# Turning the attention weights of heads 0 to 5 on DVE and through DRAM, and summing squares on ACT, in a two-layer attention and recurrence kernel

## The reference

```python
q, k, v, gate = jnp.split(rms_norm(h) @ w_in, 4, axis=-1)
q, k = rms_norm(q per head), rms_norm(k per head)
z = q @ k.T * scale                      # 128 queries x up to 1024 keys
log_beta = log_sigmoid(z)
log_skip_j = where(causal, log_sigmoid(-z), 0.0)
log_skip = cumsum(log_skip_j, reverse=True) - log_skip_j
weights = where(causal, exp(log_beta + log_skip), 0.0)
o = weights @ v
h = h + (o * silu(gate)) @ w_out
```

## Time and profile before

| | |
|---|---|
| Median of 3 runs | 1175.18 us (1175.09 to 1175.25) |
| Span of the profiled execution | 1173.5 us |
| PE busy | 1163.8 us, 99% of the span |
| DVE busy | 796.7 us, 68% |
| ACT busy | 419.7 us, 36% |
| POOL busy | 149.8 us, 13% |
| DMA traffic | 113.51 MB |

### The profile page before, as it was taken

The page is one execution under the profiler, slowest core; times in us unless marked ns, Lnnn a source line. Parts: engine busy times, 40 slices in busy tenths (PEclk is TensorE's granted clock), DMA queues, the critical chain, the costliest instruction groups (busy, mean ns, idle before and its releaser), DMA issues. The chain is left out here.

```text
span 1173.5 us, 20148 instructions
## 1 busy us (share of the span) xinstructions
PE 1163.8 (99%) x7228; PEld 1071.4 (91%) x7228; DVE 796.7 (68%) x1612; ACT 419.7 (36%) x911; POOL 149.8 (13%) x344
## 2 busy tenths in 40 slices
PE   8999999999999999999999999999999999999998
PEld 8999999999999999888888989898999999999787
DVE  5757485766767675774444778788888888788421
ACT  5535353545445454452222222323232322222200
POOL 2422121203031211110003100000000000000000
PEclk9999999999999999999999999999999999999999
DMA  8210223223142301066632110314142421117441
GB/s 251 57 53 19 73 82 112 68 83 103 67 119 73 109 1 46 1 228 218 209 108 73 55 36 20 115 66 137 70 145 72 133 86 45 45 37 296 148 139 72
DMA packets 110659, 113.51 MB, mean 97 GB/s; under 512 B 6880, under 2 KB 86752, under 8 KB 110560
## 3 DMA queue, kind: packets, MB, share of 16 engines
q1 hardware_dynamic: 110560, 112.23, 30.1%
HBM read 79.70 MB, written 32.51 MB: 96 GB/s over the span
## 5 line engine op out<-in xcount | busy, mean ns | idle before, releaser
L28 PE MATMUL p_proj<-w_qkv_hi,ut_hi 128*128 128x384 f32 x504 | 172.0, 341 | 0.2 <-DVE ut_lo L796 0.2
L30 PE MATMUL p_proj<-w_qkv_hi,ut_lo 128*128 128x384 f32 x504 | 169.1, 336 | 0.0
L29 PE MATMUL p_proj<-w_qkv_lo,ut_hi 128*128 128x384 f32 x504 | 168.7, 335 | 0.0
L28 PE MATMUL p_proj<-w_ig_hi,next_hi 128*128 128x256 f32 x512 | 145.5, 284 | 0.0
L29 PE MATMUL p_proj<-w_ig_lo,next_hi 128*128 128x256 f32 x512 | 143.1, 279 | 0.0
L30 PE MATMUL p_proj<-w_ig_hi,next_lo 128*128 128x256 f32 x512 | 143.0, 279 | 0.0
L28 PE MATMUL p_proj<-next_hi,w_qf_hi 128*128 128x512 f32 x282 | 113.2, 402 | 0.0
L30 PE MATMUL p_proj<-next_hi,w_qf_lo 128*128 128x512 f32 x282 | 110.1, 390 | 0.0
L29 PE MATMUL p_proj<-next_lo,w_qf_hi 128*128 128x512 f32 x282 | 109.8, 390 | 0.0
L808 DVE TENSOR_TENSOR_SCAN a_skip<-a_skip,a_diagonal 128x129 f32<-128x129 f32 (+3 forms) x64 | 86.9, 1358 | 30.2 <-ACT a_beta L648 28.4
L28 PEld LDWEIGHTS p_proj<-w_ig_hi,next_hi 128*128 128x128 f32 x512 | 96.2, 188 | 0.0
(11 more groups left out here) (255 smaller groups left out, 2732.3 us busy)
## 6 DMA issues: line engine op xcount, KB each, us to landing
stage<-in_hg_w_in_dram SPq DMA_DIRECT2D x32, 512.0 KB, 4.3
stage<-in_sb_w_in_dram SPq DMA_DIRECT2D x29, 512.0 KB, 5.9
w_out_hi_scratch<-m_in SPq DMA_DIRECT2D x32, 256.0 KB, 2.1
w_out_lo_scratch<-m_in SPq DMA_DIRECT2D x32, 256.0 KB, 2.3
m_in<-mixed_scratch SPq DMA_DIRECT2D x12, 448.0 KB, 6.1
a_beta<-in_x_dram SPq DMA_DIRECT2D x8, 512.0 KB, 4.3
m_in<-in_sb_w_out_dram SPq DMA_DIRECT2D x16, 256.0 KB, 3.6
ut_hi<-w_out_hi_scratch SPq DMA_DIRECT2D x8, 512.0 KB, 8.7
```

Of the source, the lines that this page charges most:

```text
L28: pe.matmul(out, w_hi, m_hi, start=start, stop=False, skip_group_check=True)
L29: pe.matmul(out, w_hi, m_lo, start=False, stop=False, skip_group_check=True)
L30: return pe.matmul(out, w_lo, m_hi, start=False, stop=stop, skip_group_check=True)
```

## The change

In heads 0 to 5 PE no longer transposes the weights. After `weigh`, DVE transposes each 32 by 32 square in place within its partitions (`flip`, a STREAM_TRANSPOSE of (i+1)*128 columns into `skip[i % 2]`). SP (`carry`) stores that in DRAM, waits until it has landed, and loads it back in four transfers, one for each group of 32 partitions, in an order that finishes the transposition, over the buffer that `beta` was in. Two steps later ACT copies the high part (`settle_weights`) and DVE makes the low part (`refine_weights`), both from SBUF. There are three `beta` buffers in place of two, and the sigmoids of tile i wait for the low part of tile i-3. `wt_hi` and `wt_lo` have another layout: a block of 128 query columns is now read as four runs of 32. Outputs move by a step or more, to the middle of the projections of steps 4, 6, 8 and of step 0 of the next head (`mid`). Heads 6 and 7 still turn their weights on PE, in the new layout.

The sums of squares move, for all heads, from DVE to ACT (`square_raw`: two Square activations of 128 columns, each of which waits for the one before), and k is scaled in place. The loads of the weight columns from head 2 on move from SP's queue to ACT's. The halves of the output weights are split at steps 1, 2, 4, 5 in place of 5, 6, 7, 9.

```diff
     PLAIN = {"before": {i: [("scores", 0, i)] for i in range(TILES)},
-             "after": {i: ([("outputs", 0, (i - 3) // 2)] if i >= 3 and i % 2 == 1 else []) +
-                       ([("turn", 0, i - 1)] if 1 <= i <= TILES else []) for i in range(USES)}}
+             "mid": {i: ([("outputs", 0, i // 2 - 2)] if i >= 4 and i % 2 == 0 else []) +
+                        ([("settle", 0, i - 2)] if i >= 2 else [("outputs", -1, PAIRS - 1)] if i == 0 else [])
+                     for i in range(USES)},
+             "after": {}}
...
-    SPLIT_AT = [5, 6, 7, 9]
+    SPLIT_AT = [1, 2, 4, 5]
+    OUTPUTS_AT = KT // 2
...
+            def carry(h, j, group):
+
+                sp.wait_ge(flipped, TILES * h + j + 1)
+                run = (j + 1) * QUARTER
+                sp.dma_start(flips[j, :, 0:4 * run], skip[j % 2][:, 0:4 * run]).then_inc(flip_stored[j % 2], 16)
+                sp.wait_ge(flip_stored[j % 2], 16 * (PAIRS * h + j // 2 + 1))
+                for c in range(4):
...
+                    sp.dma_start(flipped_blocks(h, j)[c * QUARTER:(c + 1) * QUARTER, :, :],
+                                 flips[j, :, c * run:(c + 1) * run].rearrange("(g p) r -> p g r", g=4)
+                                 ).then_inc(carried[j % 3], 16)
...
-                        if i >= 2:
-                            act.wait_ge(weights_turned, UNITS * h + ENDS[i - 2])
...
+                            elif i >= 3:
+                                act.wait_ge(wt_ready, UNITS * h + ENDS[i - 3])
...
+            def settle_weights(h, j):
+
+                act.wait_ge(carried[j % 3], 64 * ((3, 3, 2)[j % 3] * h + j // 3 + 1))
+                if j >= 2 or not known_first(h):
+                    act.wait_ge(o_done, PAIRS * h + j // 2)
+                act.activation(slot_of(wt_hi, j), flipped_blocks(h, j), ACT.Copy).then_inc(wt_hi_ready, Z_UNITS[j])
+
+            def square_raw(n, t):
...
+                for part in range(2):
+                    if part == 1 or t >= 1 or not known_first(n):
+                        act.wait_ge(sums_ready, 2 * (NAT * n + t) + part)
+                    act.activation(squares[:, :], raw[t % 4][:, part, :], ACT.Square,
+                                   accum_out=sum_sq[t % 2][:, part:part + 1]).then_inc(sums_ready, 1)
...
+            def flip(h, i):
+
+                width = (i + 1) * P
+                dve.wait_ge(weights_ready, TILES * h + i + 1)
+                dve.transpose(skip[i % 2][:, 0:width].rearrange("p (c s i) -> p s c i", c=4, i=QUARTER),
+                              weights_of(h, i)[:, 0:width].rearrange("p (s c i) -> p s c i", c=4, i=QUARTER)
+                              ).then_inc(flipped, 1)
...
+            def refine_weights(h, j):
+
+                dve.wait_ge(wt_hi_ready, UNITS * h + ENDS[j])
+                dve.tensor_tensor(slot_of(wt_lo, j), flipped_blocks(h, j), slot_of(wt_hi, j).bitcast(F32),
+                                  ALU.subtract).then_inc(wt_ready, Z_UNITS[j])
...
+                            if kt == OUTPUTS_AT:
+                                attend(h, b, plan, "mid", i)
```

More of the change, by code:

```diff
@@ L63, in build_trunk, with link @@
         m_in = [sb(f"m_in{i}", [P, HEADS, P]) for i in range(2)]
-        def link(tag):
+        row_loaded = [ctx.enter_context(nc.semaphore(f"row_loaded{r}")) for r in range(HEADS)]
+        def link(tag, layer):
             def sem(name):
@@ L73, in link @@
                     "rows_free": sem("rows_free"),
-                    "row_loaded": [sem(f"row_loaded{r}") for r in range(HEADS)],
+                    "row_loaded": row_loaded,
+                    "row_landed": 32 * (layer + 1),
                     "stored": sem("mixed_stored"),
@@ L385, in build_attention @@
         raw = [sb(f"raw{i}", [P, 3, P]) for i in range(4)]
-        squares = [sb(f"squares{i}", [P, P]) for i in range(2)]
+        squares = sb("squares", [P, P])
         sum_sq = [sb(f"sum_sq{i}", [P, 2]) for i in range(2)]
@@ L440, in build_attention @@
         weights_ready = sem("weights_ready")
+        flipped = sem("flipped")
+        flip_stored = [sem(f"flip_stored{i}") for i in range(2)]
+        carried = [sem(f"carried{i}") for i in range(3)]
         weights_turned = sem("weights_turned")
@@ L464, in of_head, with of_plan @@
             return (h, b) if d == 0 else (h + d, 1 - b)
+        def of_plan(plan, when, h, i):
+            return [entry for entry in plan[when].get(i, []) if entry[1] >= 0 or not known_first(h)]
         def turn_events(plan, projects, first_head):
@@ L469, in turn_events @@
             for i in range(USES):
-                for when in ("before", "after"):
+                for when in ("before", "mid", "after"):
                     if when == "after" and projects and i >= 3 and i % 2 == 1:
@@ L647, in sigmoids @@
                                    scale=inv_rms[b][i][:, 2:3])
-                    act.activation(beta[i % 2][:, cols], p_z[unit % 3][:, 0:width], ACT.Sigmoid,
+                    act.activation(weights_of(h, i)[:, cols], p_z[unit % 3][:, 0:width], ACT.Sigmoid,
                                    scale=inv_rms[b][i][:, 0:1]).then_inc(sigmoids_ready, 1)
             def attend(h, b, plan, when, i):
-                for what, d, tile in plan[when].get(i, []):
+                for what, d, tile in of_plan(plan, when, h, i):
                     head, half = of_head(h, b, d)
@@ L660, in attend @@
                             copy_weights(head, tile, u, turn_bank(plan, event))
+                    elif what == "settle":
+                        settle_weights(head, tile)
                     elif what == "mixed":
@@ L732, in step @@
                             split_hi(n + 1, p)
+                    if plan is FIRST and i == USES - 1:
+                        for p in range(3):
+                            load(2, p)
                     if plan is SQUEEZED and i == USES - 1:
@@ L743, in step @@
                         gate_sigmoids(n, nb, i, t)
+                    if plan is PLAIN and i == 5:
+                        load(h + 2, 3)
+                    if plan is PLAIN and i == USES - 1 and not (isinstance(h, int) and h == HEADS - 3):
+                        for p in range(3):
+                            load(h + 3, p)
                     if splits_rows(h) and i in SPLIT_AT:
@@ L810, in weigh @@
                 dve.wait_ge(scan_done, TILES * h + i + 1)
[L811 removed]
+                weights = weights_of(h, i)[:, 0:width]
+                dve.tensor_tensor(weights, weights,
                                   skip[i % 2][:, 1:width + 1], ALU.mult).then_inc(weights_ready, 1)
+            def flip(h, i):
[4 more added lines that the diff above has]
+                              ).then_inc(flipped, 1)
             def attend(h, b, plan, when, i):
[L816 removed]
+                order = of_plan(plan, when, h, i)
                 if plan is SQUEEZED and when == "after" and i == USES - 1:
@@ L822, in attend @@
                         weigh(head, tile)
+                        if plan is PLAIN:
+                            flip(head, tile)
+                    elif what == "settle":
+                        refine_weights(head, tile)
                     elif what == "outputs":
```

132 lines of the change are left out of this document (84 added, 48 removed).

## The result

| | before | changed |
|---|---|---|
| Median, same chip | 1175.2 us | 1207.8 us |
| Span of the profiled execution | 1173.5 us | 1206.6 us |
| PE busy | 1163.8 us | 1157.1 us |
| Mean granted clock of PE | 1.00 | 0.983 |

The change makes the kernel slower by a factor of 1.0274 (95% interval 1.026 to 1.0289). The forecast, 1185.7 us with a range from 1160 to 1203, had the direction and missed the size: the added time is 33 us and not 10.5.

A forecast was written before the change was run, and what follows sets the result against it. PE was taken to bound the kernel. 6 x (5.5 waited - 4.0 saved) = +9 us, plus 1.5 for squares: 1173.5 + 10.5 = 1184.0, with the 1.7 around it 1185.7 us; range 1160 to 1203 for 8 in 10.

The forecast's parts named there:

- What PE saves: PE's 36 turns of the weights in a head, 0.11 us each: 4.0 us a head, 23.8 in six heads.
- The chain: Alternating ACT and DVE work, steps 3 to 7: low part of tile 5 at 32.4 us, PE waiting 5.5 a head.
- the forecast's time 0: The end of PE's projection in step 3 of a head, from which the forecast counted its times.
- The rule against it: Low parts on DVE and POOL instructions exclude each other: up to 0.4 us each, 1.6 a head, sum 1195.
- the one on the transfers: Carries through DRAM: tile 4's takes 7 to 8 us where 10.3 are free, so it and SP's wait are hidden.
- The slower PE after each gap: Rival: PE slow behind each gap of 4.5 us, 3 us a head, time 1204; chance 0.07.
- The squares: Squares on ACT in heads -1, 6 and 7, ahead of copies PE needs: 1.5 us, ends 0 and 5.
- The full gain: Rival: flips and squares fit and PE never waits, 1153 us; chance 0.08.
- The signs: If right: PE idle before outputs in steps 6 and 8, ACT waiting before tiles 6 and 7's sigmoids, head of 65 us.
- the signs of an error: If wrong: a head of 59.5 us, ACT's high part waiting on transfers, or granted clock below 1 behind the gaps.

The follow-up runs named there:

- x2_fill: The changed kernel with idle transposes on PE ahead of its wait at outputs 2 of heads 0 to 5: 1193.7 us, ratio 1.016.
- x11: x1_split6 with, on DVE, the low part of tile i-2 made right behind the product of tile i, ahead of the flip: 1156.2 us, ratio 0.9836.
- x12: The kernel before with only the turned weights and the output bank in quarters, outputs reading runs of 32 columns: 1175.9 us, ratio 1.0003.
- x1_split6: The changed kernel with the fourth half of the output weights split at step 6 in place of step 5: 1196.4 us, ratio 1.0178.
- x4: The kernel before with only the sums of squares moved from DVE to ACT, in all heads: 1177.1 us, ratio 1.0016.
- x5: The changed kernel with the sums of squares on DVE again: 1208.6 us, ratio 1.0275.
- x3_out_after: The changed kernel with outputs 1 and 2 at the ends of steps 6 and 8 in place of their middles: 1183.0 us, ratio 1.0058.

## Why the prediction was wrong

Against the head of 60.0 us (56.9 for head 0, which holds no outputs 3), from the windows and the waits of each head:

| head | takes | waits of PE | rest |
|---|---|---|---|
| 0 | 64.88 | 4.7 | 3.3 |
| 1 | 66.50 | 5.0 | 1.5 |
| 2 | 70.30 | 7.6 | 2.7 |
| 3 | 72.24 | 9.8 | 2.4 |
| 4 | 71.16 | 8.2 | 3.0 |
| 5 | 66.22 | 4.7 | 1.5 |
| sum | 411.3 | 40.0 | 14.4 |

Six heads of 63.50 are 381.0 before; without waits and at full clock they would be 356.9, and 3.05 of that difference only moves on, with outputs 3 of head 5, into the next head, which takes 43.09 for 40.04: PE saves 21.0. So -21.0 + 40.0 + 14.4 = 33.4, where the spans differ by 33.1. The rest is half clock: x2_fill keeps the granted clock at 1.00, and about 12.4 us of it go.

The forecast's sum had +10.5. Of the 22.6 us that it missed, 14.4 are PE at half clock, a term that stood in the sum at nothing; 11.6 are longer waits of PE behind a load of output weights, which the sum also had at nothing; and 2.8 are a saving that was counted too high. Against that, the chain's own waits are 4.7 us shorter than forecast, and 1.5 us for the squares does not show.

**What PE saves** was mis-sized: 21.0 us in place of 23.8, 3.5 a head and not 4.0. It was counted from the turns of tiles 6 and 7 alone, and the smaller groups cost less. In the kernel before, in the head from 255.98 us, the turns of tiles 0 to 7 take 0.03, 0.14, 0.27, 0.36, 0.49, 0.57, 0.70 and 0.79 us from the first one's start to the start of the matmul behind them: 3.34 for the 36, 0.093 each and not 0.11. The matmul behind a group is slower as well (0.31 for a gate matmul in place of 0.23), which the forecast's 0.88 for tile 7 includes. Summed from start to start over PE's timeline, a head of x11 spends 0.6 us less on scores than one before, but 0.2 more on outputs and 0.3 more on projections. The layout is at most a small part (x12).

**The chain** held to 0.3 us. In head 5, which has no output weights to split, the matmul behind the projection of step 3 starts at 432.08, which is the forecast's time 0; DVE's timeline gives the low parts of tiles 2 to 5:

```profile
439.77 0.54 DVE L966 TENSOR_TENSOR a_wt_lo<-a_beta,a_wt_hi 128x384 fp32r<-128x384 f32 x1
...
446.84 0.68 DVE L966 TENSOR_TENSOR a_wt_lo<-a_beta,a_wt_hi 128x512 fp32r<-128x512 f32 x1
...
454.40 0.81 DVE L966 TENSOR_TENSOR a_wt_lo<-a_beta,a_wt_hi 128x640 fp32r<-128x640 f32 x1
...
463.23 0.95 DVE L966 TENSOR_TENSOR a_wt_lo<-a_beta,a_wt_hi 128x768 fp32r<-128x768 f32 x1
```

They end at 8.2, 15.4, 23.1 and 32.1 us, where 8.5, 15.7, 23.4 and 32.4 were worked out. PE waits 0.6 at outputs 1 and 4.1 at outputs 2 (forecast 1.0 and 4.5). PE's own time fits too: in head 5 of x11, where it waits for nothing, it comes to outputs 2 at 27.0 us, where 26.9 was worked out. So the chain alone costs 4.7 us a head and not 5.5, 28.3 in six heads, as x1_split6 shows. The widths of the flips and low parts were right too: flips of 0.85, 0.98, 1.11 and 1.245 us, low parts as in these rows. The rule against it, that a low part could wait for a POOL instruction, cost the chain nothing. Where the two met it was POOL's instruction that took longer: POOL's product with `minus_half` (L1110) took 1.11 us at 439.75, beside the low part from 439.77, and 0.69 at 226.82, with no low part beside it, while all six low parts of 384 columns took 0.54 us. DVE does lose time beside POOL's product on 128 columns of `a_raw`: its product of 256 columns took 0.63 us at 278.14, with POOL's from 278.09, and 0.42 at 479.22, with none. That instruction of POOL's is nearly over when a low part of the chain begins (454.07 to 454.47, the low part from 454.40), and all six low parts of 640 columns took 0.81 us.

**The first step that failed** is the one on the transfers, that the carry "is hidden, as is the wait of SP". It followed the carries and forgot what stands between them. The change moves the fourth split from step 9 to step 5 and its load to a place behind the carry of tile 4. ACT waits for it 2.2, 4.8, 7.3 and 5.7 us in heads 1 to 4, ahead of sigmoids that are in the chain. PE's waits are 39.9 us with it and 28.3 without it: x1_split6 took that out alone and was 11.3 us faster.

**The second step that failed, and the larger,** is the sum itself, which has PE idle and gives the work behind the gaps its full pace, a term at nothing without a reason. The slower PE after each gap was there only as a rival, with a chance of 0.07: 3 us a head, 18 in all. It came to 14.4, 2.4 a head. Its evidence was turns at 0.21 us at the start and 0.11 later. The pace is the same as behind the gaps, half of full; but the windows of the kernel before give the granted clock of that stretch (2 to 8 us) as 1.00, so that no view says that it is the same thing. One of them (span, PE's busy time, granted clock):

```profile
4.00:6.00 2.00, 2.00 (x12) 1.00 0.93 265
```

The mistake was to hold it for a thing beside the forecast. The forecast itself had PE idle for 4.5 us in each head, which before never happened in this stretch, and so the price belonged in its sum. 1185.7 and 18 are 1204, about 4 us from the result, but that is partly luck: the 18 are 3.6 too many, and make up for a part of the waits and of the saving that the sum still had wrong. The Trainium skill (TensorE: Matmul & The Clock Gate, Part 1: The HAM clock gate) says that PE's clock is halved when the engine has been idle and is given back when it is busy; the trace agrees, with 0.50 of full clock from 250 to 258 us and 1.00 from 260.

**The squares** were taken at 1.5 us for three heads; x4 gives 1.8 (0.8 to 3.1) for eight in the kernel before; x5 gives nothing that shows in the changed one.

**The full gain**, 1153 us with a chance of 0.08, needed "the chain 5.5 us shorter in 32.4". The order on DVE gives just that: in head 5 of x11 the low part of tile 5 ends 26.6 us behind time 0 and not 32.1. The flips account for 4.2 of it; the rest is the gating and the splits of q and k, which no longer stand ahead of the low parts either. With the split at step 6 the kernel comes to 1156.2. The low part and not the flip is what ACT and PE wait for. The carries that follow the flips do come later by it, and ACT waits 16.3 us for them in four places, but PE only 2.2.

**The signs** named ahead: PE idle 4 to 5 us in step 8 with `a_wt_lo` as releaser, about 1 us in step 6, ACT waiting for `a_wt_lo` ahead of the sigmoids of tiles 6 and 7: all there in heads 0 and 5 (4.1 us, 0.6 us, and twice 2.6 us), which take 64.9 and 66.2 us where 65 was named. Of the signs of an error, the granted clock below 1 behind the gaps was there in all six.

## What to carry to other kernels

A forecast that leaves the busiest engine idle for some microseconds must price its clock in the same sum, not as a rival; filling the wait with work that makes nothing is a cheap test of it, and gave back 14 of 33 us here, about 12 of them clock. When a change moves one instruction of an engine's order, list every wait that now stands ahead of the chain's instructions, also those of work that has nothing to do with the chain. And before a lost gain is given up, ask in which order an engine does two things of which only one is waited for: one number and three lines turned a loss of 2.7% into a gain of 1.6%.

## What the runs showed of the hardware

The clock falls while PE stands, and the work behind the gap pays: in head 2 it is at 0.50 by 250 us, PE resumes at 253.37, and full pace is back at 259.00. It can also fall behind the gap, when PE is busy again (x3_out_after, head 1). What a gap cost behind itself did not go with its length: 3.3 us in head 0 and 1.5 in head 5 behind 4.1 us, 2.4 to 3.0 behind 6.9 to 7.0, 1.6 to 3.0 in x1_split6 behind 4.1 to 4.2, and in x3_out_after next to nothing in heads 0 and 5 behind 1.9 (0.2 and 0.1) but 1.8 in head 1 behind 2.0.

A transposition of 32 by 32 squares on DVE takes 2 to 8% longer than the subtraction of the same width (the low part): 0.445 us against 0.411 for 256 columns, 1.245 against 1.220 for 1024, from the groups of the changed kernel. A matmul whose moving operand lies in runs of 32 columns runs at nearly the pace of one with runs of 128: for 256 columns 0.118 us from start to start before, 0.120 in x12 and 0.122 in x11 (means of the 48 outputs of a head).
